# A block of two mixers on one core: the q, k and v tiles of the first head as products with x instead of with the normed x

## What is computed

```
h = rms_norm(x, norm_g)                       # x * rsqrt(mean(x*x) + 1e-6) * norm_g
q, k, v, z = split(h @ w_in, 4)               # w_in: 1024 x 8192
q = rms_norm(q per half head) / 8             # 16 heads, two halves of 64 each
k = rms_norm(k per half head)
scores, two softmaxes, their weighted difference times v, a norm per head, times silu(z), then w_out
```

## Time and profile before

| | |
|---|---|
| median of 3 runs | 1914.41 us |
| the profiled execution | 1915.09 us |
| its span, first to last instruction | 1913.3 us |
| TensorE busy | 1873.1 us, 98% |
| VectorE busy | 988.9 us, 52% |
| ScalarE busy | 815.8 us, 43% |
| GpSimd busy | 124.2 us, 6% |
| mean granted TensorE clock | 0.994 |

### The profile page before, as it was taken

How to read it: one execution, slowest core, us unless ns; L and a number is a source line. 1 busy time by engine, 2 the same in 40 slices (tenths; PEclk the granted TensorE clock), 3 DMA queues, 4 the chain that set the end, 5 groups by cost and what they waited for, 6 DMA issues and landing times.

```text
span 1913.3 us, 22366 instructions
## 1 busy us (share of the span) xinstructions
PE 1873.1 (98%) x8923; PEld 1452.5 (76%) x8923; DVE 988.9 (52%) x1764; ACT 815.8 (43%) x1325; POOL 124.2 (6%) x148
## 2 busy tenths in 40 slices
PE   7999999999999999999999999999999999999997
PEld 4666666666788788888886777677888878888886
DVE  4566667666544643333347566854434673333322
ACT  5466556656643342222324555434432342222221
POOL 0111111110001000000010011000000100000000
PEclk9999999999999999999999999999999999999999
DMA  5334334332233132222223222221023322322221
GB/s 213 147 144 150 137 143 155 143 144 99 78 118 123 69 110 99 94 96 92 99 95 117 93 72 88 84 94 34 34 96 113 121 89 99 99 93 97 97 93 62
DMA packets 56526, 201.95 MB, mean 106 GB/s; under 512 B 6478, under 2 KB 6934, under 8 KB 55784
## 3 DMA queue, kind: packets, MB, share of 16 engines
q1 hardware_dynamic: 44616, 158.32, 23.6%
q0 software_dynamic: 11808, 42.21, 6.1%
HBM read 195.23 MB, written 5.28 MB: 105 GB/s over the span
## 4 chain that ended last, share of the span: by engine, by line
PE 76%; DVE 12%; ACT 9%; issue 2%; DMA 1%; POOL 0%; DVEq 0%; SPq 0%; ACTq 0%
PE ps L1111 22%; PE ps L1114 22%; PE ps L1112 22%; ACT wH L1820 2%; DVE wL L1404 2%; PE ps L1209 2%; PE ps L1173 1%; DVE a L1533 1%; PE ps L1197 1%; DVE a L1699 1%; ACT a L1931 1%; PE ps L1185 1%; PE ps L1245 1%; PE ps L1144 1%; DVE b L1464 1%
## 5 line engine op out<-in xcount | busy, mean ns | idle before, releaser
L1111 PE MATMUL ps<-hH,wH 128*128 128x512 f32 x1592 | 649.3, 408 | 7.6 <-ACT wH L1820 5.9
L1114 PE MATMUL ps<-hH,wL 128*128 128x512 f32 x1592 | 623.7, 392 | 0.2 <-DVE wL L1404 0.2
L1112 PE MATMUL ps<-hL,wH 128*128 128x512 f32 x1592 | 622.6, 391 | 0.0
L1404 DVE TENSOR_TENSOR wL<-wr,wH 128x1024 fp32r<-128x1024 f32 (+2 forms) x285 | 345.1, 1212 | 526.7 <-ACT wH L1820 526.5
L1820 ACT ACTIVATE wH<-wr 128x1024 fp32r<-128x1024 f32 (+2 forms) x285 | 295.0, 1036 | 239.8 <-PE ps L1114 226.1
L1111 PEld LDWEIGHTS ps<-hH,wH 128*128 128x128 f32 x1592 | 299.7, 188 | 104.6 <-issue 36.2
L1114 PEld LDWEIGHTS ps<-hH,wL 128*128 128x128 f32 x1592 | 299.0, 188 | 66.2 <-DVE wL L1404 1.1
L1112 PEld LDWEIGHTS ps<-hL,wH 128*128 128x128 f32 x1592 | 300.0, 188 | 62.6 <-issue 6.2
L1111 PE MATMUL ps<-gffn,wH 128*128 128x512 f32 x400 | 157.4, 394 | 1.0 <-DVE xT L1618 1.0
L1112 PE MATMUL ps<-gffn,wH 128*128 128x512 f32 x400 | 156.3, 391 | 0.0
L1114 PE MATMUL ps<-gffn,wL 128*128 128x512 f32 x400 | 156.2, 390 | 0.0
(11 more groups left out here) (301 smaller groups left out, 2049.6 us busy)
## 6 DMA issues: line engine op xcount, KB each, us to landing
wr<-wst SPq DMA_DIRECT2D x268, 512.0 KB, 3.5
a<-wfd POOLq DMA_DIRECT2D x54, 512.0 KB, 4.7
xT<-wfd POOLq DMA_DIRECT2D x18, 512.0 KB, 7.0
wr<-wst SPq DMA_DIRECT2D x16, 384.0 KB, 3.0
xT<-xin SPq DMA_DIRECT2D x8, 256.0 KB, 4.9
xT<-xin SPq DMA_DIRECT2D x2, 1024.0 KB, 6.1
xsave<-xT SPq DMA_DIRECT2D x1, 2048.0 KB, 7.9
c<-wfd POOLq DMA_DIRECT2D x8, 256.0 KB, 3.1
```

The source lines that it names most:

```text
L1111: e.matmul(o, hi, xh[k], start=k == 0, stop=False)
L1112: e.matmul(o, hi, xl[k], start=False, stop=False)
L1114: i = e.matmul(o, lo, xh[k], start=False, stop=k == t.nk - 1)
L1404: e.tensor_tensor(dst, x, hi.bitcast(F32), ALU.subtract).then_inc(s[name], 1)
```

## The change

The step list of head 0 is written anew by `first_tiles`. ScalarE and VectorE make the two parts of X[c] times gain (r0H, r0L; the step `raw` with n = 0). The products of q, k and v of head 0 run with these, q and k in a written-out order and v behind them, v in PSUM bank 4. Squares 0 to 6 are added up by GpSimd into the tile Vn[0]; TensorE sums this total and square 7 over the partitions behind the last step of q. With rs made, VectorE evicts q, k and v by a multiplication with rs. The parts of h, which all other heads need, are made between these evictions: chunks 0 and 1, then q, chunks 2 and 3, k, chunks 4 to 7, v. SyncE's queue issues the weights of slot 0 behind X[1] and those of slot 1 behind X[3]. The vector silu(c) is made from an exponential, so that only one table of ScalarE is loaded at the start. Behind the norm of the last stage nothing is changed but names.

```diff
+    def first_tiles(self, tq, tk, tv):
+
+        free = [("rs", 0)] * 4
+        for c in range(8):
+            self.raw(0, c)
+            if c < 7:
+                free[c % 4] = self.square(0, c, v=("first", c % 4), free=free[c % 4], acc_free=("rs", 0))
+            if c in (1, 3):
+                self.add("split", j=c // 2)
+        for t in (tq, tk, tv):
+            self.slot(t, 0)
+        for c, k in ((0, 0), (0, 1), (0, 2), (0, 3), (1, 0), (1, 1), (0, 4), (1, 2), (0, 5), (1, 3), (0, 6), (1, 4), (0, 7), (1, 5),
+                     (1, 6), (1, 7)):
+            self.add("mm", t=(tq, tk)[c], k=k)
+            if (c, k) == (0, 7):
+                self.square(0, 7, v=("first", 3), free=free[3])
+        self.add("split", j=2)
+        for k in range(8):
+            self.add("mm", t=tv, k=k)
+        for t in (tq, tk, tv):
+            t.done = t.slots[-1] + 1
+        rs = self.sig("rs")
+        self.add("norm_rs", n=0, stat=2, rs=rs)
+        for name in ("nv", "nh", "nl"):
+            self.count[name] = 8
+
+        def out(t):
+            self.add("out_" + t.kind, t=t, done=t.done, rs=rs, **t.more)
+            self.add("split", j=t.slots[0] + NSPL)
+
+        self.chunks(0, 0, 2, rs)
+        out(tq)
+        self.chunks(0, 2, 4, rs)
+        yield
+        out(tk)
+        self.chunks(0, 4, 8, rs)
+        out(tv)
...
         add("start")
-        for c in range(8):
-            self.square(0, c)
-        self.norm(0, "plain")
-        add("rnd", both=[sig("rnd"), sig("rnd")])
         st = [{} for _ in range(HEADS)]
-        qk_free, rs_free = [("nl", 8)] * 4, [("nl", 8)] * 4
+        qk_free, rs_free = [("rs", 1)] * 4, [("nl", 8)] * 4
...
-            t = tile("v", 4096 + 128 * h, d=d)
+            t = tile("v", 4096 + 128 * h, 4 if h == 0 else None, d=d)
...
                 if i == 0:
-                    self.two(qk(0, 0), qk(0, 1), lambda: sq_lo(0, "q"))
-                    for step in range(16):
-                        run(step)
-                    step = 16
-                    tiles = tiles[2:]
+                    first = [qk(0, 0), qk(0, 1), v(0)]
+                    for t in first:
+                        t.rhs = "r"
+                    for _ in self.first_tiles(*first):
+                        sq_lo(0, "q")
+                    add("rnd", both=[sig("rnd"), sig("rnd")])
+                    tiles = []
...
                 e.dma_start(c5(xT, c), x_d[:, 512 * c:512 * c + 512]).then_inc(s_x[c], 16)
+                if c in (1, 3):
+                    weights(c // 2)
...
-                    if d["c"] == (0 if d["n"] == 0 else 7):
+                    if d["c"] == 7:
                         take(7)
                         bank_free[7] = ("rs", d["n"] + 1)
-                    if d["n"] > 0 and d["c"] == 7:
+                        w.wait_ge(s["first"], 16)
                         w.wait_ge(s["sqa"], d["sqa"])
                         e.matmul(ps[7][:], C("one1024"), square_sum(d["n"]), start=True, stop=False).then_inc(s["stat"], 1)
-                    if d["n"] == 0 or d["c"] == 7:
                         w.wait_ge(s["nsq"], d["nsq"])
-                        e.matmul(ps[7][:], C("one1024"), square_view(d), start=d["n"] == 0 and d["c"] == 0,
-                                 stop=d["c"] == 7).then_inc(s["stat"], 1)
+                        e.matmul(ps[7][:], C("one1024"), square_view(d), start=False, stop=True).then_inc(s["stat"], 1)
...
+                    own(e.tensor_scalar(csil, csil, 1.0, None, ALU.add, ALU.bypass))
+                    own_done()
+                    own(e.reciprocal(csil, csil))
+                    own_done()
+                    e.tensor_tensor(csil, csil, S("c"), ALU.mult).then_inc(s["csil"], 1)
...
+                elif what == "out_qk":
+                    t, d2 = d["t"], d["d"]
+                    if t.rhs == "r":
+                        w.wait_ge(s["slot"], t.done)
+                        w.wait_ge(s["rs"], d["rs"])
+                        e.tensor_tensor(qk_raw[d2["m"] % 4], ps[t.bank][:], norm_views(0)[0], ALU.mult).then_inc(s["qe"], 1)
...
-                    if d["h"]:
+                    if t.rhs == "r":
+                        e.tensor_tensor(vT0, ps[t.bank][:], norm_views(0)[0], ALU.mult).then_inc(s["ve"], 1)
+                    else:
                         w.wait_ge(s["vt"], d["h"])
-                    e.tensor_copy(vT0, ps[t.bank][:]).then_inc(s["ve"], 1)
+                        e.tensor_copy(vT0, ps[t.bank][:]).then_inc(s["ve"], 1)
...
                 elif what == "start":
+                    e.preload_act_table_set("natural_log_exp_and_others")
                     w.wait_ge(s["small"], 16)
-                    e.activation(csil, S("c"), ACT.Silu).then_inc(s["csil"], 1)
+                    e.activation(csil, S("c"), ACT.Exp, scale=-1.0)
                     w.wait_ge(s["lam"], 2)
                     e.activation(lame, ps[5][:, 0:2], ACT.Exp).then_inc(s["lam"], 1)
```

More of the change, by code:

```diff
@@ L142, in __init__ @@
         self.ffn(2, "ffn2_w_in_2", "ffn2_w_out_2")
-        self.norm(4, "out")
+        self.out_norm()
     def sig(self, name):
@@ L182, in whole @@
                 then()
-    def two(self, t0, t1, then=None, ahead=False):
-        self.slot(t0, 0)
-        self.slot(t1, 0)
-        for k in range(8):
-            self.add("mm", t=t0, k=k)
-            self.add("mm", t=t1, k=k)
-        for t in (t0, t1):
-            t.done = t.slots[-1] + 1
-            if ahead:
-                self.add("split", j=t.slots[0] + NSPL)
-        for t in (t0, t1):
-            self.add("out_" + t.kind, t=t, done=t.done, **t.more)
-            if not ahead:
-                self.add("split", j=t.slots[0] + NSPL)
-            if t is t0 and then is not None:
-                then()
     def raw(self, n, c):
@@ L2146, in _ @@
             for what, d in steps:
-                if what == "square" and d["n"] > 0:
+                if what == "square":
                     c, acc, v = d["c"], square_sum(d["n"]), square_view(d)
```

145 lines of the change are left out of this document (58 added, 87 removed).

## The result

The changed kernel takes 1923.77 us (median of 5 runs, 1923.14 to 1925.7); beside it on the same chip the kernel before takes 1914.49 (median of 5, 1914.0 to 1915.57). The ratio is 1.0049, 95% interval [1.0034, 1.0063]: slower by 9 us. The prediction was slower by 5.9, with 1915.0 to 1925.0 as its range.

The account below looks back on a forecast made before the run. TensorE's work plus its standstills was taken as the bound. The point behind the sums moves +4.9, the clock adds 1.5, a credit takes 0.5: +5.9 us on 1914.41, so 1920.3, range 1915.0 to 1925.0.

Parts of the forecast that it names:

- The one fixed point: First ordinary TensorE product behind head 0's two pairs of sums, at 44.65 us before; delays there pass to the end one to one.
- Part 1, rs: Start of the kernel: VectorE and GpSimd take turns, last raw at 21.1, rs at 26.3, 9.3 us later than before.
- The credit of 0.5: Taken off part 1: VectorE ends 0.55, not 0.67, behind each of GpSimd's six additions.
- additions cost nothing: Rival for the start: GpSimd's additions cost VectorE nothing, rs at 22.0, total about 1916.5; chance 0.15.
- The distance table: GpSimd's table in the stretch of the additions: costs VectorE nothing; by the skill's rule some 0.5 us later.
- Part 2, the chain behind rs: From rs to the k sums: one VectorE chain of 21.9 us, sums at 48.2 against 44.10, bounds 17.2 and 24.
- the two waits: VectorE stands 2.3 us at the weight split behind each eviction of q and k, waiting for ScalarE's high part.
- The rival without standing time: VectorE's chain behind rs runs its 17.2 us without a stop; with earliest rs -3.0, 1911.4; chance 0.10.
- Part 3, the clock: After some 13 us idle TensorE restarts at 1.2 GHz: sums take 1.8 instead of 0.9, then 1.5 us lost.
- The rival with 1.2 GHz through all products of q and k: TensorE stays at half clock in the early products; rs at 31.8, +5.5 us more, 1925.8; chance 0.12.
- Part 4, the failed step: First ada product of head 1: fourth weight lands at 53.6, product due at 54.4, so no wait.
- a rival of 0.08: The ada weights land 2.5 us later than reckoned, sharing DMA engines with slots 6 and 7; costs up to 2, 1922.

Follow-up runs that it names:

- e8: Changed kernel with additions on VectorE, three ada transfers at rs, the fourth at the seventh chunk, and head 0's splits, roundings and evictions reordered; 1909.12 us, 0.9969 of the kernel before.
- e9: e8 with the additions of squares back on GpSimd; 1911.56 us, 0.9979 of the kernel before.
- e1: Changed kernel with GpSimd's six additions left out, so rs has other values; 1921.58 us, 1.0033 of the kernel before.
- e2: Changed kernel with the six additions made by VectorE instead of GpSimd; 1923.31 us, 1.0039 of the kernel before.
- e5: Changed kernel with the split of weight slot 3 moved ahead of the row factor's product; 1922.84 us, 1.0038 of the kernel before.
- e6: Changed kernel with roundings and first low parts of squares ahead of chunks 4 to 7, and three ada transfers at rs; 1920.05 us, 1.0024 of the kernel before.
- e4: e3 with fifteen unread matmuls of constants on TensorE ahead of the sums; 1921.41 us, 1.0032 of the kernel before.
- e3: Changed kernel with three of the four ada weight transfers issued at rs, not when h is complete; 1923.72 us, 1.0042 of the kernel before.
- e7: Changed kernel with x ahead of all weight slots in SyncE's queue; 1927.99 us, 1.0067 of the kernel before.
- e11: Changed kernel with only the fifteen unread matmuls ahead of the sums, ada transfers unmoved; 1922.40 us, 1.0038 of the kernel before.
- e10: e8 with all four ada weight transfers issued together at chunk 7's row factor product; 1911.88 us, 0.9985 of the kernel before.

## Why the prediction was right, and where it was not

**What bounds the kernel.** Held. The one fixed point was well chosen in kind, but the marker behind `ada` would have been the better one: between the two lay the step that failed.

**Part 1, rs.** Last `raw` reckoned for 21.1, measured 21.24; q7 23.1 and 23.2; use of rs 26.3 and 26.52. That the first of these comes out to the tenth is in part luck: six turns of 1.15 (6.9) were reckoned. In the trace the first addition (7.67) ran while VectorE stood still for 1.37 waiting for the high part of slot 0 (9.23); the other five held VectorE up for 5.3, and the distance table, put at nothing, for 0.3. Together 7.0. The turns of VectorE and GpSimd are shown: `raw` 1.78 against 0.75 beside the additions, all at 0.75 in e8, where they are gone (and the table is moved behind rs), and rs 2.67 later when the additions alone come back (e9). The credit of 0.5 was not paid. The rival "additions cost nothing" put rs at 22.0. e1 made the additions free and rs came at 25.17: that rival left out that TensorE itself can be slow until 15.8. Two causes of like size lay over each other, and taking one away gave 1.35 in that execution and 2.9 in e2, where the clock rose at 13.1.
The distance table was put at nothing. VectorE's `raw` of 19.48, shortly behind the table's start at 19.10, took 1.09; in e1 and e2 the one beside the table's start took 0.99 and 1.10. So it costs about 0.3, once, against the 0.75 of the earlier trace rows, which began 1.19 into a table instruction and overlapped only its last 0.43. The Trainium skill (GPSIMD Engine Reference, Key points) has contention of GpSimd with VectorE instructions of two SBUF inputs and no exception for the table; that there is some, these rows confirm. The Trainium skill says elsewhere (SBUF — State Buffer, section SBUF: two separate sides) that whoever comes first holds the shared ports for its whole instruction and the other one blocks. For the additions the rows fit this roughly: the `raw` of 16.09 took 1.77, 0.75 of work and 1.02 of standing. For the table they do not: it ran for 1.81 from 19.10, and the `raw` that met it lost 0.34, not the 1.4 that were left of it. Starts and ends on GpSimd are rough in the profile, so only the times on VectorE count for much here.

**Part 2, the chain behind rs.** Reckoned 21.4 from rs to the rounding that frees the q sums, measured 22.1 (26.52 to 48.63), with the two waits at 2.31 and 2.30, exactly as said. The idle time was forecast at 13, measured 13.91. e5 took one wait and one split out and the sums moved by 2.9; e6 changed only what stands ahead of what (and when three weights are issued) and moved them by 8, of which 7.4 lie behind rs. That the 72 early products run in time that is lost afterwards is what the gap of 13.91 shows, and e8 shows the other side: with the chain shortened from 22.1 to 7.2 (24.57 to 31.75), the same early products are worth 8.2 us at the marker. The rival without standing time did not occur.

**Part 3, the clock.** Right in kind, too large behind the point: reckoned 1.5, measured 0.6, because the half clock ended 3.1 us behind the start of the sums and not 5.9. With the 0.6 of the sums (1.84 against the 1.23 of e4) it cost 1.3 in all. The executions of e3 and e6 show that the 0.6 is no constant: they lost 1.1 and 1.9 there (4.55 and 5.39 for the five steps, against 3.49). The rival with 1.2 GHz through all products of q and k did not occur: the clock rose between 13.1 and 16.0 us in each of the kernels with the new first tiles, but for e7 (18.1), where all comes 3.7 later.

**Part 4, the failed step: "No wait, but the margin is below 1 us".** TensorE reached `ada` at 54.63, as reckoned (54.4). The weights did not land at 53.6: the fourth was issued at 48.64, not 47.4, and took 8.5, not 6.2. The term was put at 0 and measured 1.7. I had listed it as a rival of 0.08 with up to 2 us; the size was right, the chance too small. The range of landings (3.8 to 6.2) came from four transfers that had the DMA engines to themselves; here a weight slot was issued 0.35 ahead of the fourth and shared them (1.3 of the 2.3 that the landing is longer, by the estimate above), and the end came in a trickle. In e11 and e5, with the same five transfers, the fourth took 7.6 and 9.0. e3 took the wait away (1.83 for the `ada` matmuls), e10 put one back in an earlier place (4.3).

**The sum.** Forecast +5.9 (1920.3); measured +9.3 (1923.77), inside the range and 1.2 below its upper end. Marker: +8.2, that is +0.7 for rs (26.5 in place of 25.8, the credit), +0.7 for the chain, -0.9 for the clock, +1.7 for the weights. Behind the marker the profile gives -0.3: the lost clock -2.0, the wait for c +1.3, the remainder +0.4. The last 1 us, between 8.2 and 9.3, is not settled. Compared through their ratios, the kernels with the new first tiles, the combined ones too, stand 0.8 to 2.6 higher against the kernel before than their marker alone would put them, e1 and e11 excepted (-0.5 and -1.2). A longer wait for c could be behind it; which share it has in the runs without a profile no experiment here shows.

## What to carry to other kernels

Work moved ahead of a wait is worth nothing as long as another engine's list behind that wait decides when the next stage may start: read that engine's list, and shorten it first. Here the same early products cost 9 us with a chain of 22.1 us behind rs and won 6 us with one of 7.2, by nothing but the order of splits, evictions and roundings, by who adds, and by when the weights are issued. Two waits that end within 1 us of each other count as two: reckon a transfer's landing with all that is issued beside it, and take both away together, or part of the first one's gain is lost in the second.

## What the runs showed of the chip

- An addition of 128x512 f32 took 0.68 on VectorE. On GpSimd it took 1.80 beside VectorE's two-input instructions, and each of these then took 1.77 to 1.87 in place of 0.75. Six additions moved to VectorE made VectorE itself finish 2.4 us earlier (18.8 against 21.24).
- From the first product to the first matmul at full pace it took 3.6 us in e11 and 5.2 in the changed kernel, which are the same up to there, and 5.3 and 6.5 in e8 and e10, which are the same too. Behind the idle time before the sums it took 3.1 us in the changed kernel and 5.7 in e6. This one size scatters by 1 to 3 us, as much as most single edits here bring.
- A 512 KB transfer of GpSimd's queue, issued as the last of four, landed after 6.2 us when the four were alone, and after 7.6 (e11), 8.5 (the changed kernel) and 9.0 (e5) with one more of SyncE's queue beside them. The DMA engines were full in both cases (0.95 and 0.96).
- The granted clock fell for a while near 650, near 1020 to 1060 and near 1300 us, in each execution at one to three of these places, and this cost 3.4 to 7.0 us of full speed.
